# Output projections of the C heads: residual added on TensorE by a product with the identity, sums copied by ScalarE

## What is computed

```python
mix = jnp.concatenate([oc.reshape(b, t, C_W), od.reshape(b, t, D_W)], -1)
return jnp.einsum('btn,nd->btd', mix, w_out), new_c, new_d, dki
...
x = layer_norm(ALPHA * x + mix, g[0], b[0])
return layer_norm(ALPHA * x + swiglu(x, w_ffn_in, w_ffn_out), g[1], b[1])
```

## Time and profile before

| | |
|---|---|
| median of 3 runs | 3198.34 us (3196.57 to 3202.15) |
| profiled execution | 3200.3 us, of which 3198.5 us are the span of the trace |
| TensorE busy, whole span | 2978.8 us (93%) |
| VectorE busy, whole span | 1421.8 us (44%) |
| ScalarE busy, whole span | 930.3 us (29%) |
| C stages, first output projection to the barrier behind C4 | 1722.6 to 2016.4 us |

### The profile page before, as it was taken

How to read it: one execution, slowest core, us unless ns; L and a number is a source line. 1 busy time by engine, 2 the same in 40 slices (tenths; PEclk the granted TensorE clock), 3 DMA queues, 4 the chain that set the end, 5 groups by cost and what they waited for, 6 DMA issues and landing times.

```text
span 3198.5 us, 47585 instructions
## 1 busy us (share of the span) xinstructions
PE 2978.8 (93%) x17994; PEld 2782.8 (87%) x18097; DVE 1421.8 (44%) x3335; ACT 930.3 (29%) x2279; POOL 772.7 (24%) x403
## 2 busy tenths in 40 slices
PE   7999999989999999998868787899989999999997
PEld 6999999979999999997646665888779999999995
DVE  3667444143222332225389987444462233222224
ACT  3777766131000000002432332344440000000014
POOL 2000002224333334431011111111123333433330
PEclk9999999999999999999776666899999999999999
DMA  5121122101111111110000010101001111111111
GB/s 145 52 80 58 55 64 97 60 27 47 47 46 46 46 39 42 50 46 17 12 19 17 18 31 1 27 18 32 14 27 47 46 46 39 46 52 40 45 33 54
DMA packets 209707, 138.13 MB, mean 43 GB/s; under 512 B 28082, under 2 KB 189554, under 8 KB 209586
## 3 DMA queue, kind: packets, MB, share of 16 engines
q1 hardware_dynamic: 208930, 136.27, 14.3%
q10 hardware_dynamic: 656, 0.26, 0.0%
HBM read 116.77 MB, written 19.71 MB: 43 GB/s over the span
## 4 chain that ended last, share of the span: by engine, by line
PE 80%; DVE 13%; ACT 4%; issue 2%; DMA 0%; POOL 0%; DVEq 0%; ACTq 0%; POOLq 0%
PE ps L1082 21%; PE ps L1084 21%; PE ps L1083 21%; DVE sel_mask L2070 5%; PE ps L1373 3%; PE ps L1194 3%; PE ps L1471 2%; DVE Y L2246 1%; PE ps L1352 1%; PE ps L1106 1%; PE ps L1340 1%; PE ps L1341 1%; PE ps L1561 1%; DVE yc L2438 1%; DVE Hl L2472 1%
## 5 line engine op out<-in xcount | busy, mean ns | idle before, releaser
L1082 PE MATMUL ps<-Xh,w_hi 128*128 128x352 f32 (+3 forms) x3216 | 1056.3, 328 | 38.1 <-DVE Xl L2443 24.9
L1084 PE MATMUL ps<-Xh,w_lo 128*128 128x352 f32 (+3 forms) x3216 | 1041.8, 324 | 0.0
L1083 PE MATMUL ps<-Xl,w_hi 128*128 128x352 f32 (+3 forms) x3216 | 1041.3, 324 | 0.0
L913 POOL TENSOR_TENSOR w_hi<-w_raw,zero 128x1024 fp32r<-128x1024 f32 x154 | 292.9, 1902 | 1757.5 <-PE ps L1084 1186.4
L1082 PEld LDWEIGHTS ps<-Xh,w_hi 128*128 128x128 f32 (+1 forms) x3216 | 608.9, 189 | 44.7 <-issue 31.2
L1083 PEld LDWEIGHTS ps<-Xl,w_hi 128*128 128x128 f32 (+1 forms) x3216 | 610.2, 190 | 1.0
L1084 PEld LDWEIGHTS ps<-Xh,w_lo 128*128 128x128 f32 (+1 forms) x3216 | 608.6, 189 | 0.5
L2470 DVE TENSOR_TENSOR hid_f<-ps,gate_s 128x352 f32<-128x352 f32 x132 | 69.2, 524 | 770.5 <-PE ps L1084 770.5
L915 POOL TENSOR_TENSOR w_lo<-w_raw,w_hi 128x1024 fp32r<-128x1024 f32 x154 | 374.8, 2434 | 12.1
L1082 PE MATMUL ps<-Hh,w_hi 128*128 128x352 f32 x1056 | 343.5, 325 | 9.7 <-DVE Hl L2472 9.7
L1084 PE MATMUL ps<-Hh,w_lo 128*128 128x352 f32 x1056 | 341.2, 323 | 0.0
(11 more groups left out here) (231 smaller groups left out, 3679.7 us busy)
## 6 DMA issues: line engine op xcount, KB each, us to landing
w_raw<-in_w_ffn_in_dram SPq DMA_DIRECT2D x176, 256.0 KB, 3.1
w_raw<-in_w_ffn_out_dram SPq DMA_DIRECT2D x88, 256.0 KB, 2.8
w_raw<-in_w_in_even_dram SPq DMA_DIRECT2D x48, 256.0 KB, 3.3
w_raw<-in_w_in_odd_dram SPq DMA_DIRECT2D x26, 256.0 KB, 3.4
x_in<-in_x_prompt_dram SPq DMA_DIRECT2D x8, 512.0 KB, 8.9
w_raw<-in_w_out_even_dram SPq DMA_DIRECT2D x16, 256.0 KB, 3.3
w_raw<-in_w_out_odd_dram SPq DMA_DIRECT2D x16, 256.0 KB, 3.1
out_dram<-Y SPq DMA_DIRECT2D x8, 512.0 KB, 2.7
```

What stands on the lines that cost most here:

```text
L913: pool.tensor_tensor(view(WH[w][:, :]), raw, zeros, ALU.add).then_inc(S["w_split"], 1)
L1082: pe.matmul(out, wh, hi, start=first, stop=False)
L1083: pe.matmul(out, wh, lo, start=False, stop=False)
L1084: return pe.matmul(out, wl, hi, start=False, stop=last)
```

## The change

The 24 jobs of each C output projection get a fourth product: the identity, in 32-bit floats, by the piece of `Y` that the job belongs to, added in PSUM to the three others. ScalarE, not VectorE, then copies the sum from PSUM to `Y`. In C2 ScalarE's copies of the transposed values and keys are put between the copies of the sums, in the order in which TensorE issues them. VectorE's additions remain for the D heads. The semaphore `dve_ev` is renamed `y_ev` everywhere, and ahead of a C projection's first job TensorE waits until all earlier writes to `Y` are done.

```diff
-                            pe.wait_ge(S["dve_ev"], at_down("dve_ev", j - 2))
-
-                        mm = three(ps[:, D_BANKS[(at_down.static("jobs") + j) % 3], 0:CH], slot(at_down, 0), m,
-                                   M[att].OTh[:, c * CH:(c + 1) * CH], M[att].OTl[:, c * CH:(c + 1) * CH], True, True)
+                            pe.wait_ge(S["y_ev"], at_down("y_ev", j - 2))
+
+                        if att == "C" and j == 0:
+                            pe.wait_ge(S["y_ev"], at_down("y_ev"))
+                        out = ps[:, D_BANKS[(at_down.static("jobs") + j) % 3], 0:CH]
+                        mm = three(out, slot(at_down, 0), m, M[att].OTh[:, c * CH:(c + 1) * CH],
+                                   M[att].OTl[:, c * CH:(c + 1) * CH], True, att != "C")
+                        if att == "C":
+                            mm = pe.matmul(out, ident[:, :], Y[:, m, c * CH:(c + 1) * CH], start=False, stop=True)
                         mm.then_inc(S["d_done"], 1)
...
-            def key_value_rows(at, kind):
-
-                act.wait_ge(S["stores"], at("stores"))
+            def key_value_rows(at, kind, groups):
+
+                if 0 in groups:
+                    act.wait_ge(S["stores"], at("stores"))
                 new_t = NT + CACHE[kind]
-                for g, (what, tiles) in enumerate(KV_GROUPS[kind]):
+                for g in groups:
+                    what, tiles = KV_GROUPS[kind][g]
...
-                if kv:
-                    key_value_rows(at_proj, proj)
+                groups = range(len(KV_GROUPS[proj]) if kv else 0)
+                if att != "C":
+                    if kv:
+                        key_value_rows(at_proj, proj, groups)
+                    return
+                for j in range(3 * KB):
+                    m, c = j // 3, j % 3
+                    if c == 0 and m in groups:
+                        key_value_rows(at_proj, proj, [m])
+                    act.wait_ge(S["d_done"], at_down("jobs", j + 1))
+                    act.activation(Y[:, m, c * CH:(c + 1) * CH], ps[:, D_BANKS[(at_down.static("jobs") + j) % 3], 0:CH], ACT.Copy)\
+                        .then_inc(S["y_ev"], 1)
...
-                if att:
+                if att and att != "C":
                     for j in range(3 * KB):
                         m, c = j // 3, j % 3
                         dve.wait_ge(S["d_done"], at_down("jobs", j + 1))
                         cs = slice(c * CH, (c + 1) * CH)
                         dve.tensor_tensor(Y[:, m, cs], ps[:, D_BANKS[(at_down.static("jobs") + j) % 3], 0:CH], Y[:, m, cs],
-                                          ALU.add).then_inc(S["dve_ev"], 1)
+                                          ALU.add).then_inc(S["y_ev"], 1)
                         if kv and j % 3 == 2 and j // 3 in split_groups:
                             cached_low(at_proj, proj, j // 3)
-                elif kv:
+                elif kv and not att:
                     for g in split_groups:
                         cached_low(at_proj, proj, g)
```

More of the change, by code:

```diff
@@ L129, in reciprocal_step @@
     return 2 * (t + 1) if kind == "C" else t + 1
-DOWN_PART = dict(units=1, jobs=3 * KB, dve_ev=3 * KB, ot_done=len(TM_ALL), oth=len(TM_ALL), otl=len(TM_ALL))
+DOWN_PART = dict(units=1, jobs=3 * KB, y_ev=3 * KB, ot_done=len(TM_ALL), oth=len(TM_ALL), otl=len(TM_ALL))
 def add(*parts):
@@ L145 @@
 LN_PART = dict(ln_mm=6, ln_yc=3, ln_sq=3, ln_sd=3, ln_rs=3, ln_xn=3, ln_x=24, ln_xh=3, ln_lo=3)
-FFN_PART = dict(units=6, jobs=12 + 3 * KB, dve_ev=3 * KB, gate=6, hid=6, hidh=6, hidl=6)
+FFN_PART = dict(units=6, jobs=12 + 3 * KB, y_ev=3 * KB, gate=6, hid=6, hidh=6, hidl=6)
 N_IDX = len(INDEX_TILES)
@@ L149 @@
                relu=4 * N_IDX, acc=4 * N_IDX, dve=N_IDX - 1)
-SETUP_INC = dict(w_split=4, d_done=36, act_ev=1, dve_ev=6, pv=1, soft=1, onorm=1, stores=16)
+SETUP_INC = dict(w_split=4, d_done=36, act_ev=1, y_ev=6, pv=1, soft=1, onorm=1, stores=16)
 X_GROUPS = 2 * (NT + 1)
-SETUP_PART = dict(tgroups=X_GROUPS, units=2, jobs=36, act_ev=1, dve_ev=6, pv=1, soft=1, onorm=1, stores=16)
+SETUP_PART = dict(tgroups=X_GROUPS, units=2, jobs=36, act_ev=1, y_ev=6, pv=1, soft=1, onorm=1, stores=16)
 EV_KINDS = "AAAABBBB"
@@ L477, in build @@
         o_park = nc.dram_tensor("o_park", [len(EV_KINDS), 2, P, T], F32).ap()
-        names = ["w_split", "d_done", "act_ev", "dve_ev", "t_done", "t_ev", "scores", "soft",
+        names = ["w_split", "d_done", "act_ev", "y_ev", "t_done", "t_ev", "scores", "soft",
                  "ot_done", "low", "cache_hi", "negmax", "exps", "probs", "pv", "onorm", "oth", "otl", "bias_ld", "bias_ok", "rms",
@@ L1488, in up @@
                     elif j < 6:
-                        pe.wait_ge(S["dve_ev"], at("dve_ev", j - 5))
+                        pe.wait_ge(S["y_ev"], at("y_ev", j - 5))
                     elif j < 9:
@@ L2481, in group @@
                             ins = dve.tensor_tensor(Y[:, m, cs], ps[:, j % 6, 0:CH], Y[:, m, cs], ALU.add)
-                        ins.then_inc(S["dve_ev"], 1)
+                        ins.then_inc(S["y_ev"], 1)
                 group(At(f"F{l}"), True)
```

## The result

The changed kernel takes 3227.09 us (median of five runs, 3218.69 to 3228.96) against 3200.50 us (median of five, 3196.57 to 3203.81) of the kernel before. The ratio on record is 1.0063, with a 95% interval of 1.0048 to 1.0079: slower by 15 to 25 us. It is not the quotient of these two medians, which is 1.0083, or 26.6 us. Timed again beside the experiments, the changed kernel took 3224.69 us against 3207.33 us, a ratio of 1.0055 (1.0035 to 1.0075). So it is slower, clear of the noise, by some 20 us. The forecast was 3218 us, 3209 to 3241, slower. The profiled execution takes 3227.61 us, its span 3225.8 us.

The account below looks back on a forecast made before the run. The prediction took the C stages to be bound by VectorE's selection parts and additions, with TensorE stalling behind them. Stage terms +6.5 - 8.3 + 7.1 + 14.4 = +19.7 us, added to 3198.34, gave 3218 us, range 3209 to 3241.

Parts of the forecast that it names:

- What bounds the stages: C stages: VectorE's selection parts and additions before; TensorE last after, VectorE idle some 19 us in C1 and C3, 6 in C2.
- x: Time of one plain 32-bit identity product on TensorE in a C output job, taken as 0.598 us from LayerNorm's rows.
- Rival 4: In C output jobs operand kinds don't mix freely: x = 0.82 us, +41 us, 3239 us; upper bound within the 0.79 case.
- C1 and C3: Stretches from first output job to next scores, set by TensorE's 24 jobs of 25.9 us: +6.5 and +7.1 us.
- C2: Stretch from first output job to next scores: -8.3 us, TensorE ending 5.7 us after the selection parts.
- C4: Last C stage, up to the barrier: nothing stalled, nothing hidden, identity products added whole, +14.4 us.
- The copies: 96 copies from PSUM moved to idle ScalarE, 0.46 us each: cost nothing; only the barrier waits for the last one.
- The clock: TensorE's granted clock in C1 to C3: assumed to stay at 1.00 through the new stream of jobs.
- rival 3: Mixed products drop TensorE's clock: 2.16 us a job, 3244 us for one stage, 3320 us for all four; chance 0.06.
- The sum: Changes of the four C stretches together, 96x - 37.7 in general: +19.7 us.

## Why the prediction was right, point by point

- *What bounds the stages.* Right. Before, VectorE; after, TensorE, with VectorE idle for 19.57, 3.53 and 21.56 us ahead of the scores of the three stages, where "some 19" and 6 were said.
- *x.* LayerNorm's rows gave 0.598 us; the chain shows 0.59, and the kernel without the product 0.585 to 0.594. The row of the same operand type and shape was the right one to price by, though it computes something else; the split products in the same job were the wrong one by a factor of 3.7. Rival 4 fell with it: the two kinds in one sum cost nothing that shows beside the 0.59. (The timeline has it in two places: 0.32 us from the first identity record to the next job's first product, and 0.43 instead of 0.16 from that product to the second, 0.27 more; together 0.59.)
- *The page "FP8 and Floating Point Precision"* of the Trainium skill (section "TensorE Precision Notes"), with its four passes for a true 32-bit product, agrees in size with the 0.59 us, for which the prediction's estimate from it was 0.587. That there are four passes no row shows; the profile has two records. The Trainium skill's page "TensorE: Matmul & The Clock Gate" (section "Back-to-back issue gap") gives its formula for an isolated product and speaks of no operand type; this case does not bear it out for plain 32-bit operands: by its figure the stretches would have come to an estimated 15.2 us, 24 x (0.483 + 0.149), and they are 26. (By the prediction's own stage sums that price makes an estimated -18.3 us in all, not the -19 that it gives.)
- *C1 and C3*: +6.56 and +7.25 us, forecast +6.5 and +7.1.
- *C2*: -8.63 us, forecast -8.3. The sum held; the margin in it did not hold in every execution. In the trace shown above the selection parts end 23.8 us after the first job and VectorE then idles for 3.53 us, where 21.3 and 5.7 were said. In the second trace of the same kernel the first job starts at 1835.83, the parts end 21.3 us after it, and VectorE idles for 5.97 us:

```profile
1856.98 0.17 DVE L2092 COPY_PREDICATED threshold<-enough,trial 128x7 int32<-128x7 int32 x1
...
1863.13 0.06 DVE L2134 MEMSET carry<- 1x1 f32 x1 [5.97 <-PE ps L1161]
```

  The stretch is 26.66 us both times. The offset of the parts' end against the first job is 21.0 to 23.8 us over the nine traces and differs between two executions of one kernel, so it does not go with the edits. In the first trace VectorE comes to the low split of C2 straight from a selection part, and the five parts behind it begin to count 9.1 us ahead of the first job (1824.77); in the second VectorE waits 1.02 us for ScalarE's part of the split, and still they begin 11.6 us ahead (1824.27). What makes VectorE later in the first was not followed further back. The selection would have ended the stage with x below 0.59 - 3.53 / 24 = 0.44 us in the first trace, and below 0.34 in the second.
- *C4*: +13.8 us, forecast +14.4. The step said that the first 4.6 us run at a granted clock of 0.50 both times. In the changed kernel they are fewer:

```profile
2011.90:2015.50 3.60, 3.54 (x9) 2.94 (x10) 0.79 (x2) 0.56 (x3) 0.00 (x0) 0.50 0.00 0
2015.50:2016.00 0.50, 0.50 (x3) 0.28 (x2) 0.00 (x0) 0.00 (x0) 0.00 (x0) 0.76 0.00 0
2016.00:2016.50 0.50, 0.50 (x5) 0.50 (x4) 0.00 (x0) 0.33 (x1) 0.00 (x0) 1.00 0.00 0
```

  (Windows of the changed kernel: stretch, length, busy us by engine, granted clock, DMA share, GB/s.) The high level is there after some 3.7 us, before it was after some 4.7; one microsecond less at half speed is 0.5 us, an estimate. In the second trace of the changed kernel it is there after some 4 us, and the stretch is 28.57.
- *The copies*: 465 ns, 61.6 us of ScalarE idle ahead of the 96, nobody waits for them but the barrier. Right.
- *The clock* (rival 3): 1.00 through all three stretches, C1 to C3:

```profile
1728.90:1755.10 26.20, 25.99 (x120) 20.67 (x120) 7.20 (x20) 10.85 (x25) 0.00 (x0) 1.00 0.00 1
1833.80:1860.50 26.70, 26.70 (x130) 21.15 (x127) 23.38 (x61) 12.84 (x29) 0.00 (x0) 1.00 0.09 23
1926.00:1952.10 26.10, 26.10 (x121) 20.73 (x121) 4.48 (x9) 11.25 (x25) 0.00 (x0) 1.00 0.00 1
```

- *The sum*: +19.0 us in the stretches, +19.3 between the two second traces, forecast +19.7. That the median lies 9 us above the forecast is not in a step of it: 2 us are the kernel before, whose median went from 3198.34 to 3200.50 with two more runs, and 6 us of the profiled difference arise before the change begins, which no step had. How many of the timed runs hold those 6 us is not on record, so it is in part chance that the ratio's +20 us meets the forecast so closely; the stretches are what bears it out.

## What to carry to other kernels

Price a product by a row with the same operand types and shape: a plain 32-bit product of 352 columns cost 0.59 us where a split one cost 0.16, so an addition of 0.524 us on another engine is not cheaper on TensorE. What a moved operation gives back is the stall that it caused in each stage, not its own duration: the same edit was worth -8.6 us in C2 and +13.8 in C4, and used only for as many jobs as TensorE can do while VectorE selects it made a kernel 20.5 us faster than before. Moving the sum without moving the emptying of its bank gives nothing back: with VectorE's copies the change cost 47 us, not 20.

## What was not expected of the hardware

The stage D0, the indexer's scores for the D heads, lies ahead of the C output projections, and yet takes some 6 us longer in the changed kernel: the dense projection behind it starts at 1619.84, before at 1612.99. From there to the first C output job the two kernels differ by 0.4 us (109.27 and 109.63). The windows at its end show where. Kernel before, changed kernel, and the kernel without the identity product (columns as in the windows above: the third figure from the end is the granted clock):

```profile
1600.00:1604.00 4.00, 3.49 (x10) 1.46 (x10) 2.62 (x4) 2.74 (x4) 0.00 (x0) 0.96 0.00 0
1608.00:1614.00 6.00, 4.07 (x18) 1.92 (x17) 5.29 (x20) 2.45 (x4) 0.00 (x0) 1.00 0.00 1
```

```profile
1600.00:1604.00 4.00, 4.00 (x9) 2.00 (x8) 1.95 (x3) 1.83 (x2) 0.00 (x0) 0.50 0.00 0
1608.00:1614.00 6.00, 6.00 (x11) 1.89 (x11) 3.05 (x3) 2.57 (x3) 0.00 (x0) 0.50 0.00 0
```

```profile
1600.00:1604.00 4.00, 3.79 (x9) 1.75 (x8) 1.84 (x2) 1.37 (x3) 0.00 (x0) 0.50 0.00 0
1604.00:1608.00 4.00, 3.50 (x10) 1.43 (x10) 2.59 (x4) 2.74 (x4) 0.00 (x0) 0.95 0.00 0
```

The granted clock is at its low level, 0.50 or 1.2 GHz, through most of D0; while the score products run it rises to the high one at about 1600 us in the first, at about 1604 in the third, and not at all before D0 ends in the second. Of nine profiled executions three show the early rise (both of the kernel before, and the one without the identity product; 239.8 to 240.1 us from LayerNorm to the first C job), one a late rise (243.1 us), and five none (246.1 to 246.5 us; both of the changed kernel among them). The kernel without the identity product runs the changed kernel's code up to C1 and has the rise, so that code does not exclude it. But both traces of the kernel before have it and both of the changed one do not, so whether the change makes it rarer stays open. Runs of which no trace is left show that the kernel before varies without any edit: its 28 runs beside the experiments took 3196.55 to 3213.28 us, with a mean granted clock of 0.944 to 0.937, by and large the lower the longer the run; where in the program that lies is not on record. It is 6 us that no edit of the C stages has been shown to explain, and it bears on how an effect of 20 us is read from one pair of profiles: in stretches, not in spans.
